# Output weights in the entries of two mixers: late loads behind the next heads, earlier splits, Pool's low parts in pieces of 256 columns, tails by halves

## The chip, the core and the metric

The kernel runs as one program on one core of a Trainium2 chip. The core has a matmul engine (TensorE, PE in the profile; PEld is its loading of stationary tiles), VectorE (DVE), ScalarE (ACT), GpSimd (Pool, POOL) and SyncE (SP, which here issues all DMAs, on one queue). Compute engines work on SBUF (128 partitions) and, all but Pool, on PSUM; each runs its own instruction stream and waits on semaphores. The metric is device microseconds of one execution, median of several runs.

## The reference

One inference step of a two-layer recurrent decoder, width 1024, for a prompt of 1040 tokens (16 of them learned) and for 8 samples of 4 tokens each. Layer 0 has four mLSTM heads and an RG-LRU, layer 1 four heads of gated linear attention (GLA). Each layer is a norm, an input projection, a mixer that carries states, an output projection and a second norm:

```python
hn = _rmsnorm(x, pre_g)
proj = jnp.einsum('bld,de->ble', hn, w_in)
...                                   # layer 0: q, k, v, gates of 4 mLSTM heads; RG-LRU channels
hm = _head_norm(sigmoid(og) * hm, m_norm_g, M_HEADS) * silu(z)
mix = jnp.concatenate([hm, hl * silu(gr)], axis=-1)          # 2048 features
...                                   # layer 1, chunk by chunk
o = qd @ S + causal(qd @ kd.T) @ v
S_new = exp(bL) * S + (k * exp(bL - b)).T @ v
mix = _head_norm(o, g_norm_g, G_HEADS) * silu(r)             # 2048 features
...
out = jnp.einsum('ble,ed->bld', mix, w_out)                  # w_out: 2048 x 1024
y = x + _rmsnorm(out, post_g)
```

All of it is float32, and the new states of prompt and samples are outputs too.

## The kernel before

Five stages stand in a row for each layer's norm, projection and mixer, with barriers between them. A float32 product is made of three products of rounded parts: each operand x is split into a high part (x rounded, a ScalarE copy) and a low part (x minus the high part, a subtraction on VectorE or Pool), and PE multiplies high by high, high by low and low by high.

The mixers (`stage_mix_a` for layer 0, `stage_mix_c` for layer 1) run 36 steps: 9 chunks of 128 tokens (the last holds 16 prompt tokens and the 32 sample tokens) by 4 heads. In step n PE turns and multiplies the next head (`part_a(n + 1)`), makes half of the output projection of head n - 1 (`out(n - 1, 0)`), a unit of the samples' state work (`unit`), the other half (`out(n - 1, 1)`), turns the normed head (`part_c(n)`) and makes the next head's products (`part_b(n + 1)`). Each engine's stream is written out by hand in this order.

SP loads heads two steps ahead into two buffers: step n + 2's head goes when `b_done` says that step n's products are made (`load_head`). At the start of a mixer it loads the second head, the first states, the post-norm row and the residual, some sample inputs, and the late weights.

The output weights (class `OutRing`) are 16 row tiles of 128 x 1024. Some are loaded during the projection (8 in A, 10 in C: `early`), the rest at the start of the mixer (`late`, two tiles, 1 MB, to a DMA: four DMAs in A, three in C; `load_late`). They are split in four groups k of four tiles, in the order in which the first four heads need them: ScalarE makes the four high parts (`split_w_hi`, L1407), VectorE two low parts (`split_w_lo`, L1413), Pool the other two, each in one instruction of 1024 columns (`split_w_lo_pool`, L1420). Group 0 is split before the loop of steps in A and within step 0 in C; group k = n + 1 at the end of step n.

In A, VectorE's chain of a step is: the state's update, the numerator, a division in three small operations on one column (`divide`, L2072 to L2076 with the gating), the norm with ScalarE, the scaling of the normed head (L2082), and the samples' read and update (L2065); PE's `part_c` waits for the scaling and the update. Pool makes the low parts of each head's mix (L2228, L2233) and the masked sample queries (L2238). In C, Pool scales each state after its update (`scale_state`, L3158), makes the mix's low part (`lo`, L3165), and in the beginning builds masks (13 linked operations from L3137 on), the samples' decayed keys (`sample_head`, L3172) and the low parts of six stacks (`stack_lo`, L3204), which PE turns around its first products (`first_turn`, L2801).

The last chunk's output (48 rows) is normed in `tail_act` and `tail_dve`: high and low contributions lie in separate rows of PSUM, ScalarE copies the low ones to SBUF by halves of 512 columns, VectorE adds, ScalarE squares and takes the root, VectorE scales and adds the residual.

Of the kernel before, what the change touches and what calls it, by code (L numbers as in the profile page):

```python
# [21 lines left out]
D = 1024  # L22
# [1332 lines left out]
class OutRing:  # L1355
# [40 lines left out]
    def raw(self, e):  # L1396
        w = self.early if e in self.early.list else self.late
        return w.rows[:, w.list.index(e), :]

    def split_w_hi(self, act, k):  # L1400

        for e in self.order[4 * k:4 * k + 4]:
            if e in self.late.list:
                act.wait_ge(self.late_in[self.late.list.index(e) // 2], 16)
            else:
                act.wait_ge(self.early.loaded, 16 * self.early.tiles // 2)
            act.activation(self.w_hi[:, e, :], self.raw(e), ACT.Copy).then_inc(self.w_hi_ready, 1)  # L1407

# [7 lines left out]
    def split_w_lo_pool(self, pool, k):  # L1416
        for j in range(2, 4):
            e = self.order[4 * k + j]
            pool.wait_ge(self.w_hi_ready, 4 * k + j + 1)
            pool.tensor_tensor(self.w_lo(e), self.raw(e), self.w_hi[:, e, :].bitcast(F32), ALU.subtract  # L1420
                               ).then_inc(self.w_ready_pool, 1)

# [70 lines left out]
    def tail_act(self, act, ps, buf):  # L1493

        for half in range(2):
            act.wait_ge(self.m_used, self.used(4 * NC - 1) - 1 + half)
            act.activation(buf[0:LAST, half * 512:half * 512 + 512], ps[64:64 + LAST, 6 + half, :], ACT.Copy).then_inc(self.tail_low, 1)
        for half in range(2):
            act.wait_ge(self.tail_sum, half + 1)
            act.activation(ps[0:LAST, 6 + half, :], buf[0:LAST, half * 512:half * 512 + 512], ACT.Square,  # L1500
                           accum_out=self.stat[0:LAST, half:half + 1]).then_inc(self.squares, 1)
        self.root(act, 8, LAST)

    def tail_dve(self, dve, ps, buf):
        st = self.stat
        for half in range(2):
            x = buf[0:LAST, half * 512:half * 512 + 512]
            dve.wait_ge(self.tail_low, 2)
            dve.tensor_tensor(x, ps[0:LAST, 6 + half, :], x, ALU.add).then_inc(self.tail_sum, 1)
        dve.wait_ge(self.squares, 18)  # L1510
        dve.tensor_tensor(st[0:LAST, 2:3], st[0:LAST, 0:1], st[0:LAST, 1:2], ALU.add).then_inc(self.sq_sum, 1)
        dve.wait_ge(self.post_rstd, 2 * NC)
        dve.scalar_tensor_tensor(out=buf[0:LAST, :], in0=buf[0:LAST, :], scalar=st[0:LAST, 4:5], in1=self.post[0:LAST, :],
                                 op0=ALU.mult, op1=ALU.mult).then_inc(self.scaled, 1)
        dve.wait_ge(self.scaled, 17)
        dve.wait_ge(self.x_in, 16 * NC)
        dve.tensor_tensor(self.yx[0:LAST, :], buf[0:LAST, :], self.yx[0:LAST, :], ALU.add).then_inc(self.y_ready, 1)

# [37 lines left out]
def stage_mix_a(nc, S, scr_d, lru_d, row_d, w_early, w_late, post_d, x_d, y_d, c0_d, out_cp, out_cs, first):  # L1556
    with ExitStack() as ctx:
# [130 lines left out]
        with nc.Block() as block:  # L1688
            @block.sync
            def _(sp):  # L1690
# [49 lines left out]
                load_state(0)  # L1740
                O.load_late(sp)
                projected(3)
# [5 lines left out]
                for n in range(NSTEP):  # L1748
# [5 lines left out]
                    if n + 1 < UNITS:  # L1754
                        load_state(n + 1)
                    u = unit_of(n)
                    if u is not None:
# [819 lines left out]
def stage_mix_c(nc, S, scr_d, w_early, w_late, post_d, x_d, y_d, s0_d, out_sp, out_ss, first):  # L2577


    with ExitStack() as ctx:  # L2580
# [114 lines left out]
        with nc.Block() as block:  # L2695
            @block.sync
            def _(sp):
# [44 lines left out]
                O.load_x(sp, 0, P)  # L2742
                O.load_late(sp)
                load_sample_r(0)
                load_sample_head(1)
                for n in range(NSTEP):
# [3 lines left out]
                    if n + 2 < NSTEP:  # L2750
                        load_head(n + 2)
                    if 0 < n < UNITS:
                        load_state(n)
# [164 lines left out]
            def _(act):  # L2918
# [62 lines left out]
                def part_m(n):  # L2981
                    c, h, rows = where(n)
                    act.wait_ge(mp_ready, n + 1)
                    if n >= 2:
                        act.wait_ge(O.m_used, O.used(n - 2))
                    x = mp[:].rearrange("p (d t) -> p d t", d=4) if c < 8 else mp8[:, 4 * h:4 * h + 4, :]
                    act.activation(O.hi(n, 0, 4), x, ACT.Copy).then_inc(mhi_ready, 1)
                copy_v(0)
                for j in range(7):
                    if j < 6:  # L2990
                        stack_hi(0, j)
                    if j:
                        aux_copy(0, j - 1)
                for s in range(2):
                    act.wait_ge(S.spilled[s], C_SPILLED[3])
                for n in range(NSTEP):
                    c, h, rows = where(n)
                    norm(n)
                    if n + 1 < NSTEP:
                        copy_v(n + 1)  # L3000
                    if n == 0:
                        O.split_w_hi(act, 0)
                    item = early_aux(n)
# [24 lines left out]
            def _(dve):  # L3028
# [66 lines left out]
                def part_m(n):  # L3095
# [6 lines left out]
                                      ALU.mult).then_inc(mp_ready, 1)  # L3102
                part_a(0)
                dve.wait_ge(pool_chain, POOL_LINKS)
                for n in range(NSTEP):
# [7 lines left out]
                    if n == 0:  # L3113
                        group_keys(0)
                        O.split_w_lo(dve, 0)
                    if u is not None:
# [18 lines left out]
            def _(pool):  # L3135
                link = linker(pool, pool_chain)
                link(pool.memset(qm[:].bitcast(F32), 0.0))  # L3137
                for t in range(3):
                    part = mask_k[t * NS:(t + 1) * NS, :]
                    link(pool.memset(part, 1.0))  # L3140
                    link(pool.affine_select(out=part, in_=part, compare_op=ALU.is_ge, fill=0.0,
                                            base=0, pattern=[[-SLEN, NSEQ]], channel_multiplier=1))
                    link(pool.affine_select(out=part, in_=part, compare_op=ALU.is_ge, fill=0.0,
                                            base=SLEN - 1, pattern=[[SLEN, NSEQ]], channel_multiplier=-1))
                link(pool.memset(mask_s[:], 1.0))
                link(pool.affine_select(out=mask_s[:], in_=mask_s[:], compare_op=ALU.is_ge, fill=0.0,
                                        base=0, pattern=[[1, NS]], channel_multiplier=-1))
                part = mask_s[:].rearrange("p (s t) -> p s t", t=SLEN)
                link(pool.affine_select(out=part, in_=part, compare_op=ALU.is_ge, fill=0.0,
                                        base=0, pattern=[[-SLEN, NSEQ], [0, SLEN]], channel_multiplier=1))  # L3150
                assert link.count() == POOL_LINKS

                def scale_state(n):
# [51 lines left out]
                sample_head(0)  # L3205
                for j in range(6):
                    stack_lo(0, j)
                first_q()
                for n in range(NSTEP):
                    c, h, rows = where(n)  # L3210
                    u = unit_of(n)
                    scale_state(n)
                    if n == 0:
                        O.split_w_lo_pool(pool, 0)
                    if n + 1 < NSTEP:
# [183 lines left out]
```

## Time and profile before

| quantity | value |
| --- | --- |
| median of 3 runs | 2133.11 us (2132.53 to 2135.07) |
| the profiled execution's own time | 2130.55 us |
| its span, first to last instruction | 2128.7 us |
| PE busy | 2037.7 us (96%) |
| DVE / ACT / POOL busy | 1321.2 / 841.3 / 275.3 us |
| mean granted clock of PE | 0.979 of full speed |
| DMA | 264.35 MB, mean 124 GB/s |

Mixer A lies between about 695.6 and 1091 us of the span, mixer C between about 1664.9 us and the end. PE counts as busy while a matmul is in its pipeline, so a busy PE is not PE at its peak. In a timeline a line is one instruction, or several merged (x2, x4), with its start, its duration, and in brackets how long its engine idled before it and what it waited for; an instruction that has started but stands for a memory port counts as busy.

### The profile page before, as it was taken

Reading aid. Unit: us, or ns where it says so; the run is one execution under the profiler, and the core shown is the slowest. Engines: PE = TensorE matmul, PEld = TensorE weight load, DVE = VectorE, ACT = ScalarE, POOL = GpSimd, SP = SyncE. Lnnn points to the kernel's source line nnn. Section 1 sums busy time; section 2 is a strip of 40 time slices with the busy share of each in tenths; the row PEclk is TensorE's granted clock in tenths of the full one; section 3 lists DMA queues with packets and bytes.
Section 4 is the critical chain, followed back from the end, with each engine's and each line's share of the span. In section 5 each row is a group of like instructions: output and inputs, shape, how many; then the busy total and the mean of one; then the engine's idle time right before and its main releaser. Section 6 shows DMA issues by size and latency. Waiting matters only on the chain. (4 is left out here: it accounts for less than half of the span.)

```text
span 2128.7 us, 32848 instructions
## 1 busy us (share of the span) xinstructions
PE 2037.7 (96%) x12606; PEld 1830.4 (86%) x12606; DVE 1321.2 (62%) x2263; ACT 841.3 (40%) x1535; POOL 275.3 (13%) x382
## 2 busy tenths in 40 slices
PE   7999999999999699999959999999999799999998
PEld 7999999999999578788749999999999677777774
DVE  5466676645665676776656656776655576566664
ACT  5555543323231444444455434332212353344333
POOL 0000000000000421111100000000000453333222
PEclk9999999999999799999979999999999899999999
DMA  3121133443343554555332232344333544545442
GB/s 139 55 65 65 53 95 92 132 151 103 101 122 89 204 157 151 161 165 163 102 125 75 81 93 81 121 152 142 107 99 113 183 166 158 180 166 177 161 152 72
DMA packets 209221, 264.35 MB, mean 124 GB/s; under 512 B 48228, under 2 KB 156004, under 8 KB 207032
## 3 DMA queue, kind: packets, MB, share of 16 engines
q1 hardware_dynamic: 209080, 262.42, 38.5%
q8 instruction: 95, 1.56, 0.3%
q14 instruction: 46, 0.38, 0.1%
HBM read 172.39 MB, written 89.99 MB: 123 GB/s over the span
## 5 line engine op out<-in xcount | busy, mean ns | idle before, releaser
L568 DVE TENSOR_TENSOR pa_stage<-pa_ps,pa_stage 128x536 f32<-128x536 f32 x110 | 77.1, 713 | 122.6 <-PE pa_ps L535 112.1
L568 DVE TENSOR_TENSOR pc_stage<-pc_ps,pc_stage 128x536 f32<-128x536 f32 x110 | 77.1, 713 | 98.3 <-PE pc_ps L535 78.3
L382 PE MATMUL pa_ps<-a_XT_hi,pa_w_hi 128*128 128x358 f32 x576 | 133.2, 340 | 0.3 <-PEq L201 0.3
L382 PE MATMUL pa_ps<-a_XT_hi,pa_w_lo 128*128 128x358 f32 x576 | 125.9, 327 | 0.0
L382 PE MATMUL pa_ps<-a_XT_lo,pa_w_hi 128*128 128x358 f32 x576 | 125.8, 326 | 0.0
L535 PE MATMUL pc_ps<-c_XT_hi,pc_w_hi 128*128 128x268 f32 x384 | 110.2, 287 | 0.0
L535 PE MATMUL pa_ps<-a_XT_hi,pa_w_lo 128*128 128x268 f32 x384 | 110.1, 287 | 0.0
L535 PE MATMUL pc_ps<-c_XT_hi,pc_w_lo 128*128 128x268 f32 x384 | 110.1, 287 | 0.0
L535 PE MATMUL pc_ps<-c_XT_lo,pc_w_hi 128*128 128x268 f32 x384 | 110.1, 287 | 0.0
L535 PE MATMUL pa_ps<-a_XT_lo,pa_w_hi 128*128 128x268 f32 x384 | 110.0, 286 | 0.0
L535 PE MATMUL pa_ps<-a_XT_hi,pa_w_hi 128*128 128x268 f32 x384 | 109.8, 286 | 0.0
L1449 PE MATMUL mc_ps<-mc_wout_hi,mc_mix_hi 128*128 128x512 f32 x256 | 105.8, 413 | 2.6 <-POOL mc_mix_lo L3165 2.6
L1449 PE MATMUL ma_ps<-ma_wout_hi,ma_mix_hi 128*128 128x512 f32 x256 | 105.5, 412 | 0.1
L382 PEld LDWEIGHTS pa_ps<-a_XT_hi,pa_w_hi 128*128 128x128 f32 x576 | 100.2, 189 | 5.9 <-issue 0.6
L1449 PE MATMUL ma_ps<-ma_wout_hi,ma_mix_lo 128*128 128x512 f32 x256 | 100.9, 394 | 0.0
L1449 PE MATMUL mc_ps<-mc_wout_hi,mc_mix_lo 128*128 128x512 f32 x256 | 100.8, 394 | 0.0
L1449 PE MATMUL mc_ps<-mc_wout_lo,mc_mix_hi 128*128 128x512 f32 x256 | 100.7, 393 | 0.0
L1449 PE MATMUL ma_ps<-ma_wout_lo,ma_mix_hi 128*128 128x512 f32 x256 | 100.4, 392 | 0.0
L382 PEld LDWEIGHTS pa_ps<-a_XT_hi,pa_w_lo 128*128 128x128 f32 x576 | 99.6, 189 | 0.0
L382 PEld LDWEIGHTS pa_ps<-a_XT_lo,pa_w_hi 128*128 128x128 f32 x576 | 99.4, 189 | 0.0
L3158 POOL TENSOR_TENSOR mc_state<-mc_state,gf 128x512 f32<-128x512 f32 x72 | 75.0, 1062 | 98.3 <-DVE mc_state L3056 98.3
L382 PE MATMUL pc_ps<-c_XT_hi,pc_w_hi 128*128 128x358 f32 x384 | 84.4, 328 | 0.3 <-PEq L201 0.3
(589 smaller groups left out, 6122.7 us busy)
## 6 DMA issues: line engine op xcount, KB each, us to landing
pa_w_raw<-in_w_a SPq DMA_DIRECT2D x57, 512.0 KB, 4.6
pc_w_raw<-in_w_c SPq DMA_DIRECT2D x49, 512.0 KB, 4.5
scr_c<-pc_stage SPq DMA_DIRECT2D x48, 512.0 KB, 3.2
scr_a<-pa_stage SPq DMA_DIRECT2D x40, 512.0 KB, 3.2
mc_sample_state<-in_s SPq DMA_DIRECT2D x32, 512.0 KB, 4.5
out_s_s<-mc_sample_state SPq DMA_DIRECT2D x32, 512.0 KB, 2.7
ma_sample_state<-in_c SPq DMA_DIRECT2D x32, 257.0 KB, 4.1
out_c_s<-ma_sample_state SPq DMA_DIRECT2D x32, 257.0 KB, 2.9
```

The costliest lines, as they stand in the source:

```text
L382: ins = pe.matmul(self.ps[:, 3 * s + t, 0:TC], w[:, k, :], x[:, k, t * TC:(t + 1) * TC], start=(k == 0 and j == 0), stop=(k == KT - 1 and ...
L535: ins = pe.matmul(bank[:, half, :], a[:, k, :], b[:, k, cols], start=(k == 0 and j == 0), stop=(k == KH - 1 and j == 2))
L568: dve.tensor_tensor(dst, self.out(p, product), x, ALU.add).then_inc(self.added, 1)
L1449: ins = pe.matmul(ps[:, 6 + half, :], m[:, at, :], w, start=first and j == 0, stop=last and j == 2)
L3158: ins = pool.tensor_tensor(cst[:, h, d, :], cst[:, h, d, :], factor, ALU.mult)
```

## The change

SP's late loads move behind the loads of step 0 of the loop: in A behind step 2's head and its companions, in C behind step 2's head. Pool's low part of a weight tile is four instructions of 256 columns instead of one of 1024, in both mixers. In C group 0 is split earlier on all three engines: ScalarE's high parts one by one between the copies of the first stacks, VectorE's low parts in front of its wait for the masks, Pool's in front of the loop and so of the first `scale_state`; Pool's decayed keys and its first two stacks stand in front of the masks, and ScalarE's first stack in front of the copy of v. In the tails each half is copied, added, squared and multiplied by the post-norm row on its own, and the last pass over 1024 columns does the root's factor and the residual in one operation. All weights, sums and results are the same; the products by factors are taken in another order in the tails.

```diff
--- before.py
+++ after.py
@@ class OutRing @@
+    def split_w_hi_one(self, act, k, j):
+        e = self.order[4 * k + j]
+        if e in self.late.list:
+            act.wait_ge(self.late_in[self.late.list.index(e) // 2], 16)
+        else:
+            act.wait_ge(self.early.loaded, 16 * self.early.tiles // 2)
+        act.activation(self.w_hi[:, e, :], self.raw(e), ACT.Copy).then_inc(self.w_hi_ready, 1)
+
     def split_w_hi(self, act, k):
...
+        for j in range(4):
+            self.split_w_hi_one(act, k, j)
...
     def split_w_lo_pool(self, pool, k):
         for j in range(2, 4):
             e = self.order[4 * k + j]
             pool.wait_ge(self.w_hi_ready, 4 * k + j + 1)
-            pool.tensor_tensor(self.w_lo(e), self.raw(e), self.w_hi[:, e, :].bitcast(F32), ALU.subtract
-                               ).then_inc(self.w_ready_pool, 1)
+            for cols in (slice(q * D // 4, (q + 1) * D // 4) for q in range(4)):
+                ins = pool.tensor_tensor(self.w_lo(e)[:, cols], self.raw(e)[:, cols], self.w_hi[:, e, cols].bitcast(F32), ALU.subtract)
+            ins.then_inc(self.w_ready_pool, 1)
...
@@ tail_act @@
             act.activation(buf[0:LAST, half * 512:half * 512 + 512], ps[64:64 + LAST, 6 + half, :], ACT.Copy).then_inc(self.tail_low, 1)
-        for half in range(2):
             act.wait_ge(self.tail_sum, half + 1)
...
@@ tail_dve @@
             x = buf[0:LAST, half * 512:half * 512 + 512]
-            dve.wait_ge(self.tail_low, 2)
+            dve.wait_ge(self.tail_low, half + 1)
             dve.tensor_tensor(x, ps[0:LAST, 6 + half, :], x, ALU.add).then_inc(self.tail_sum, 1)
-        dve.wait_ge(self.squares, 18)
+            dve.wait_ge(self.squares, 17 + half)
+            dve.tensor_tensor(x, x, self.post[0:LAST, half * 512:half * 512 + 512], ALU.mult).then_inc(self.scaled, 1)
         dve.tensor_tensor(st[0:LAST, 2:3], st[0:LAST, 0:1], st[0:LAST, 1:2], ALU.add).then_inc(self.sq_sum, 1)
         dve.wait_ge(self.post_rstd, 2 * NC)
-        dve.scalar_tensor_tensor(out=buf[0:LAST, :], in0=buf[0:LAST, :], scalar=st[0:LAST, 4:5], in1=self.post[0:LAST, :],
-                                 op0=ALU.mult, op1=ALU.mult).then_inc(self.scaled, 1)
-        dve.wait_ge(self.scaled, 17)
+        dve.wait_ge(self.scaled, 18)
         dve.wait_ge(self.x_in, 16 * NC)
-        dve.tensor_tensor(self.yx[0:LAST, :], buf[0:LAST, :], self.yx[0:LAST, :], ALU.add).then_inc(self.y_ready, 1)
+        dve.scalar_tensor_tensor(out=self.yx[0:LAST, :], in0=buf[0:LAST, :], scalar=st[0:LAST, 4:5], in1=self.yx[0:LAST, :],
+                                 op0=ALU.mult, op1=ALU.add).then_inc(self.y_ready, 1)
@@ stage_mix_a, sync @@
                 load_state(0)
-                O.load_late(sp)
                 projected(3)
...
                         load_state(n + 1)
+                    if n == 0:
+                        O.load_late(sp)
                     u = unit_of(n)
@@ stage_mix_c, sync @@
                 O.load_x(sp, 0, P)
-                O.load_late(sp)
                 load_sample_r(0)
...
                         load_head(n + 2)
+                    if n == 0:
+                        O.load_late(sp)
                     if 0 < n < UNITS:
@@ stage_mix_c, scalar @@
+                stack_hi(0, 0)
                 copy_v(0)
-                for j in range(7):
+                stack_hi(0, 1)
+                aux_copy(0, 0)
+                for j in range(2, 7):
                     if j < 6:
                         stack_hi(0, j)
-                    if j:
-                        aux_copy(0, j - 1)
+                        O.split_w_hi_one(act, 0, j - 2)
+                    aux_copy(0, j - 1)
...
-                    if n == 0:
-                        O.split_w_hi(act, 0)
@@ stage_mix_c, vector @@
                 part_a(0)
+                O.split_w_lo(dve, 0)
                 dve.wait_ge(pool_chain, POOL_LINKS)
...
                         group_keys(0)
-                        O.split_w_lo(dve, 0)
@@ stage_mix_c, gpsimd: the helpers now stand in front, unchanged @@
+                sample_head(0)
+                for j in range(2):
+                    stack_lo(0, j)
                 link = linker(pool, pool_chain)
                 link(pool.memset(qm[:].bitcast(F32), 0.0))
...
                 assert link.count() == POOL_LINKS
...
-                sample_head(0)
-                for j in range(6):
+                for j in range(2, 6):
                     stack_lo(0, j)
                 first_q()
+                O.split_w_lo_pool(pool, 0)
                 for n in range(NSTEP):
                     c, h, rows = where(n)
                     u = unit_of(n)
                     scale_state(n)
-                    if n == 0:
-                        O.split_w_lo_pool(pool, 0)
```

## Rows read from the trace of the kernel before

**Rows 1.** PE's busy tenths in the 40 slices of the page (53.2 us each).
```profile
PE   7999999999999699999959999999999799999998
```

**Rows 2.** Timeline of PE at mixer A's entry: start us, us, engine line, operation [idle before].
```profile
709.44 0.69 PE L1831 MATMUL ma_ps<-ident,ma_normed 128*128 128x128 f32 x2 [5.47 <-DVE ma_normed L2082]
...
718.25 0.47 PE L1789 MATMUL ma_ps<-ident,first_head_a 128*128 128x128 f32 x1 [2.70 <-DMA first_head_a<-scr_r]
...
728.03 0.38 PE L1831 MATMUL ma_ps<-ident,ma_normed 128*128 128x128 f32 x2
...
741.75 0.66 PE L1831 MATMUL ma_ps<-ident,ma_normed 128*128 128x128 f32 x2 [4.26 <-DVE ma_sample_state L2065]
...
755.76 0.41 PE L1831 MATMUL ma_ps<-ident,ma_normed 128*128 128x128 f32 x2 [2.23 <-DVE ma_sample_state L2065]
```

**Rows 3.** Windows: us, busy of PE, PEld, DVE, ACT, POOL, PEclk, DMA share, GB/s.
```profile
705.00:710.00 5.00, 0.56 (x2) 0.29 (x2) 3.98 (x7) 1.98 (x8) 2.08 (x1) 0.63 1.01 426
```

**Rows 4.** Timeline of SP's issues at mixer A's entry.
```profile
697.74 2.17 SPq L1235 DMA_DIRECT2D wout_a_late<-in_w_oa  x4
...
701.63 10.73 SPq L1722 DMA_DIRECT2D ma_sample_z<-scr_a  x2
712.40 0.47 SPq L1695 DMA_DIRECT2D first_head_a<-scr_a  x1
```

**Rows 5.** Timeline of VectorE in mixer A's steps 0, 1 and 4.
```profile
703.34 1.46 DVE L2072 SCALAR_TENSOR_TENSOR ma_small<-ma_num 128x1 f32<-128x1 f32 x1
704.83 2.26 DVE L2074 TENSOR_TENSOR ma_small<-ma_small,tok 128x1 f32<-128x1 f32 x1
...
725.55 0.86 DVE L2065 SCALAR_TENSOR_TENSOR ma_sample_state<-ma_sample_state,wc,ma_ps 128x257 f32<-128x257 f32 x2
...
759.66 0.16 DVE L2072 SCALAR_TENSOR_TENSOR ma_small<-ma_num 128x1 f32<-128x1 f32 x1
```

**Rows 6.** Timeline of Pool at mixer A's entry.
```profile
700.08 1.21 POOL L2238 CAST ma_q_masked<-first_head_a 128x32 fp32r<-128x32 f32 x1
...
702.44 4.64 POOL L1420 TENSOR_TENSOR ma_wout_lo<-wout_a_early,ma_wout_hi 128x1024 fp32r<-128x1024 f32 x2
710.35 0.72 POOL L2233 TENSOR_TENSOR ma_mix_lo<-ma_hl,ma_mix_hi 128x256 fp32r<-128x256 f32 x1 [3.28 <-ACT ma_mix_hi L1921]
```

**Rows 7.** Timeline of PE at mixer C's entry.
```profile
1669.80 0.66 PE L2801 MATMUL mc_ps<-ident,mc_stack 128*96 128x128 f32 x2 [2.84 <-POOL mc_stack L3204]
...
1684.90 0.44 PE L2787 MATMUL mc_ps<-ident,first_head_c 128*128 128x128 f32 x2 [2.79 <-DMA first_head_c<-scr_c]
...
1689.00 0.79 PE L1449 MATMUL mc_ps<-mc_wout_hi,mc_mix_hi 128*128 128x512 f32 x1 [2.58 <-POOL mc_mix_lo L3165]
```

**Rows 8.** Timelines of ScalarE, Pool and VectorE at mixer C's entry.
```profile
1666.99 0.60 ACT L2925 ACTIVATE mc_v_hi<-mc_ps 128x512 fp32r<-128x512 f32 x1 [21.33 <-PE mc_ps L2793]
...
1664.93 1.01 POOL L3137 MEMSET mc_q_masked<- 128x1088 f32 x1 [567.01 <-POOLq L2344]
...
1668.83 0.30 POOL L3172 TENSOR_TENSOR mc_k_decayed<-first_head_c,gf 128x64 f32<-128x64 f32 x1
...
1681.47 5.27 POOL L1420 TENSOR_TENSOR mc_wout_lo<-wout_c_early,mc_wout_hi 128x1024 fp32r<-128x1024 f32 x2 [2.98 <-ACT mc_wout_hi L1407]
1686.71 2.24 POOL L3165 TENSOR_TENSOR mc_mix_lo<-mc_mix_plain,mc_mix_hi 128x512 fp32r<-128x512 f32 x1
...
1684.45 3.38 DVE L3073 TENSOR_TENSOR mc_sample_state_lo<-mc_sample_state,mc_sample_state_hi 128x1024 fp32r<-128x1024 f32 x1 [1.64 <-ACT mc_sample_state_hi L2958]
```

**Rows 9.** Timelines of ScalarE and VectorE in mixer C's tail.
```profile
2119.88 0.59 ACT L1497 ACTIVATE first_head_c<-mc_ps 48x512 f32<-48x512 f32 x1 [0.33 <-PE mc_ps L1452]
...
2120.50 1.28 DVE L1509 TENSOR_TENSOR first_head_c<-mc_ps,first_head_c 48x512 f32<-48x512 f32 x2 [5.73 <-ACT first_head_c L1497]
...
2123.33 1.28 DVE L1513 SCALAR_TENSOR_TENSOR first_head_c<-first_head_c,mc_post_stat,mc_post 48x1024 f32<-48x1024 f32 x1 [0.60 <-ACT mc_post_stat L1467]
2124.64 1.22 DVE L1517 TENSOR_TENSOR mc_residual<-first_head_c,mc_residual 48x1024 f32<-48x1024 f32 x1
```

More of the change, by code:

```diff
@@ L1398, in raw @@
         return w.rows[:, w.list.index(e), :]
-    def split_w_hi(self, act, k):
[L1402 to L1407, printed above, removed]
+    def split_w_hi_one(self, act, k, j):
[5 more added lines that the diff above has]
+        act.activation(self.w_hi[:, e, :], self.raw(e), ACT.Copy).then_inc(self.w_hi_ready, 1)
+    def split_w_hi(self, act, k):
+        for j in range(4):
+            self.split_w_hi_one(act, k, j)
     def split_w_lo(self, dve, k):
@@ L3135, in _ @@
             def _(pool):
[L3136 to L3151, printed above, removed]
                 def scale_state(n):
@@ L3205, in _ @@
                 sample_head(0)
-                for j in range(6):
+                for j in range(2):
+                    stack_lo(0, j)
+                link = linker(pool, pool_chain)
+                link(pool.memset(qm[:].bitcast(F32), 0.0))
+                for t in range(3):
+                    part = mask_k[t * NS:(t + 1) * NS, :]
+                    link(pool.memset(part, 1.0))
+                    link(pool.affine_select(out=part, in_=part, compare_op=ALU.is_ge, fill=0.0,
+                                            base=0, pattern=[[-SLEN, NSEQ]], channel_multiplier=1))
+                    link(pool.affine_select(out=part, in_=part, compare_op=ALU.is_ge, fill=0.0,
+                                            base=SLEN - 1, pattern=[[SLEN, NSEQ]], channel_multiplier=-1))
+                link(pool.memset(mask_s[:], 1.0))
+                link(pool.affine_select(out=mask_s[:], in_=mask_s[:], compare_op=ALU.is_ge, fill=0.0,
+                                        base=0, pattern=[[1, NS]], channel_multiplier=-1))
+                part = mask_s[:].rearrange("p (s t) -> p s t", t=SLEN)
+                link(pool.affine_select(out=part, in_=part, compare_op=ALU.is_ge, fill=0.0,
+                                        base=0, pattern=[[-SLEN, NSEQ], [0, SLEN]], channel_multiplier=1))
+                assert link.count() == POOL_LINKS
+                for j in range(2, 6):
                     stack_lo(0, j)
                 first_q()
+                O.split_w_lo_pool(pool, 0)
                 for n in range(NSTEP):
```

## Prediction

> **What bounds the kernel now.** Read the busy shares by slice first: the matmul engine PE stands at nine tenths or more but for the first and last slice and three holes: slices 14, 21 and 32 [rows 1]. Slices 14 and 32 hold the entries of the two mixers, which the change touches, so the question is what PE waits for there and whether its next wait lies close behind.
>
> Entry of mixer A: PE idles 5.47 us before the first head's transposes (waiting for VectorE's normed head), 2.70 us for a DMA at step 2's part A, nothing at step 1's transposes, then 4.26 and 2.23 us at steps 2 and 3, ended by VectorE's update of the sample state [rows 2]. From 705 to 710 us the granted clock is 0.63, so part of this stretch runs at 1.2 instead of 2.4 GHz [rows 3].
>
> The DMA wait: SP issues the four late weight loads at 697.74 us, the second sample-z load is then stuck for most of 10.73 us, and step 2's head goes out only at 712.40 [rows 4]. Meanwhile the DMA engines move 426 GB/s [rows 3]: the late weights stand in front.
>
> The VectorE waits: a division on one column takes 1.46 us and the next one 2.26 us, where step 4 has 0.16 for the same line [rows 5]. They start while Pool runs its two low parts of output weights, 2.32 us each [rows 6]; the second division ends at 707.09, with Pool's second piece (702.44 + 4.64 = 707.08). So a VectorE operation with both inputs in SBUF stands until the running Pool operation ends, and gets in between two of them. It also works the other way: Pool's cast of 32 columns, begun while VectorE makes its two low parts, takes 1.21 us [rows 6].
>
> Entry of mixer C: PE waits 2.84 us for Pool's first stack, 2.79 us for a head's DMA and 2.58 us for Pool's low part of the first mix [rows 7]. Pool makes its two low parts of weights from 1681.47 in 5.27 us, and only then the mix's low part (2.24 us, ending at 1688.95); VectorE's low part of a sample state takes 3.38 us meanwhile [rows 8].
>
> **Late loads in A.** Nothing is removed; four issues move behind the loads of step 2's head, row, z and sample state. Step 2's head can go when step 0's products are done, some 10 us earlier than now, with 2.5 MB at most ahead of it; PE asks for it at 715.5 at the earliest. I take the whole 2.70 us as gained. What is late next: the 4.2 MB of late weights take 9.8 us at 426 GB/s, so they land by about 716 us; the splits that read them come a step after that. Queued behind them on SP are step 3's head, which is wanted only after step 2's start, with some 5 us to spare. In C the same move ends the 2.79 us wait, but PE's next wait (Pool's low part) absorbs it: nothing by itself.
>
> **Pieces of 256 columns.** Eight instructions in place of two in each of four groups per mixer. The nearest row for a piece is Pool's own 128x256 subtraction, 0.72 us; a quarter of 2.32 is 0.58 [rows 6]. Between the two, 0.66: a group takes 5.3 instead of 4.64 us. [...]
>
> What VectorE wins: the excess of the two divisions is 1.46 + 2.26 - 2 x 0.16 = 3.4 us. With pieces, the first waits half a piece (0.33), the second a whole one (0.66), the gating behind them and the scaling of the normed head, which now meet pieces too, about 0.45 each: 1.9. I take 1.5 us gained per step. Bounds: with 0.58 and no wait behind the gating 1.1 remain (2.3 gained); with 0.72 and every operation waiting, the reciprocal too, 2.9 (0.5 gained).
>
> On PE's path: step 0 gains 1.5 (its wait ends in this chain), the DMA 2.7, together 4.2. At step 1 VectorE's update ends at 726.41 [rows 5] and PE's transposes start at 728.03 [rows 2], 1.6 us of cover; VectorE itself comes 1.5 + 1.5 earlier, so 4.6 are allowed and the 4.2 stay. Steps 2 and 3 end in VectorE's chain: 1.5 each. Entry of A: 4.2 + 3.0 = 7.2 us. Low: 3.2, cut to 1.6 + 1.0 = 2.6 at step 1, plus 1.0 = 3.6. High: 5.0 + 2.3 + 2.2 = 9.5. From step 4 on PE runs without waits, so what is gained is kept.
>
> **Early splits and Pool's order in C.** ScalarE's four high parts move into the gaps of the first turns, VectorE's two low parts in front of its wait for the masks, Pool's eight pieces in front of the first scaling of the state. The key scaling and two stacks go in front of the masks: PE's 2.84 us wait goes, and its first products can start about 1 us earlier than now, once VectorE has v's low part. But Pool waits for the second stack's high part, which ScalarE makes behind the copy of v (1666.99 to 1667.59), so the masks start at about 1668.1 instead of 1664.93 and still need the 3.9 us that lie before 1668.83 [rows 8], till 1672. VectorE's two low parts (about 2.4 us) now fall upon them. By the cast that took 1.21 [rows 6] the masks' selects wait for these: stack 2 comes at 1674.3, in the middle of PE's first products, which end 1.5 us later than now. Then stacks and first queries till 1678, the pieces till 1683.6, the state's scaling, now in front of the mix (2 us), till 1685.7, and VectorE's low parts of state and weight take the port in between: the first mix's low part is there between 1687 and 1689.3, against 1688.95 today. The 5.6 us that Pool starts earlier are spent on scaling, pieces and contention. I take 0.5 us gained; bounds 2 lost and 4 gained (masks free of VectorE's low parts).
>
> The page SBUF — State Buffer of the Trainium skill (Who interferes with whom) says that the port pair shared by VectorE and GpSimd is an exclusive lock held for a whole instruction, and that a GpSimd instruction which only writes does not contend. By that rule the masks' memsets pass and the selects, which read, stand as I assume; no row here shows a select that met VectorE's low part.
>
> **Tails by halves.** Now both copies end at 2120.47, both sums at 2121.78, and the two last passes take 1.28 + 1.22 us [rows 9]. After: ScalarE squares half 0 before it copies half 1; sum and square (0.64 and about 0.65, with handing over 1.4) take the place of the 0.33 us for which it waits for PE today, so that copy ends 1.05 later; the second sum, behind the first multiplication, ends at 2122.3, 0.55 later; the multiplication of half 1 (0.64) stands in front of the tiny addition that the root waits for; then one pass of 1.28 remains. 0.55 + 0.64 - 1.25 = 0, in both tails; bounds 0.3 either way.
>
> **Sum.** 7.2 + 0.5 + 0 = 7.7 us off the profiled execution's own 2130.55: 2122.9. The median of the runs shown, 2133.11, lies 2.56 above it: 2125.4 us. A measurement of this kernel can tell about 0.2%, 4.3 us, from no change: under 2128.8 is faster.
>
> **Rivals.**
> - The port is freed more fully and the masks are not held up: A gains 9.5, C 3: 2120.6. For it: divisions of 0.16 us slip between two Pool pieces without lengthening them. Against: the cast's 1.21.
> - Mixer C pays: Pool's longer chain and PE's lost time at 1.2 GHz in its longer first wait cost 2 us, while A gains its low 3.6: 2131.5, no change. For it: Pool has scaling and pieces in front of the first mix. Against: Pool starts 5.6 us earlier.
> - The DMA wait moves: step 3's head lands behind the late weights, 2.7 us come back: 2128.1. For it: SP's stuck issue today. Against: the 5 us to spare.
> - Slower: Pool holds the port over its train of pieces, so that a division waits for all eight, at 0.72 each 5.8 us in place of 4.64. That is 1.1 us later on each of VectorE's chains: A's step 1 overruns its cover (2.2 - 1.6 = 0.6), steps 2 and 3 lose 2.2, and C's first two mixes 2: 2133.1 + 4.8 = 2137.9. It decides if the second division still takes over 2.3 us. Against it: today VectorE gets in between two Pool instructions.
>
> **Chances.** Forecast 0.45, fuller gain 0.23, moved wait 0.10 (all three faster); C pays 0.16 (same); train 0.06 (slower). Faster 0.78, same 0.16, slower 0.06. The likeliest case alone spans 2122 to 2128; the range for 8 in 10 reaches from A's and C's high ends (13.5 us) to the low end of A with C losing: 2119 to 2131.
>
> **What the changed profile would show.** Right: no DMA wait at A's step 2, SP issuing that head before the late weights; divisions of 0.3 to 0.9 us in steps 0 to 3, Pool's pieces 0.6 to 0.75; PE's waits at steps 2 and 3 of A shorter by 1.5 to 3 us in sum; step 4 of A about 7 us earlier. In C, Pool's masks stretched to 5 or 6 us and the first mix's low part at about the old time from the stage's start. The tails' last passes one instead of two, and the end no earlier against the last product. Wrong, if the second division keeps over 2 us, if a new DMA wait stands at step 3, or if C's first output products start 3 us earlier or 2 later.

## The result, and the profile after

The changed kernel takes 2121.75 us (median of 4 runs, 2119.16 to 2124.78) against 2134.09 us before: ratio 0.9943, 95% interval 0.993 to 0.9955, 12.3 us faster. The forecast was 2125.4, that is 7.7 us faster, in a range from 2119 to 2131. The profiled execution has a span of 2117.4 us (before 2128.7). Cut at the same marks, the 11.3 us between the two spans lie here (the marks are start times in the timelines, but for two: A's tail ends with its last pass, and the last row with the span):

| stretch | before | after | difference |
| --- | --- | --- | --- |
| start to mixer A's first transpose | 695.63 | 696.37 | +0.74 |
| A's entry: first transpose to step 3's normed head | 60.13 | 48.00 | -12.13 |
| rest of A with its tail | 335.37 | 335.25 | -0.12 |
| layer C's norm and projection | 573.84 | 573.33 | -0.51 |
| mixer C: first transpose to its last product | 454.47 | 455.22 | +0.75 |
| last product to the end | 9.26 | 9.23 | -0.03 |

The first and the fourth row are stretches that the change does not touch; over all profiles here they lie between 694.4 and 696.6, and 573.3 and 577.0. So the gain is A's entry. Mixer C's 0.75 us is less than what the same streams of C differ by between profiles: its entry, to step 3's normed head, took 57.95 us here, 57.57 in a second profile of this kernel and 56.25 in another kernel with the same C (57.22 before).

The page of the changed kernel, PE's slices and the granted clock [rows 1]:

```profile
PE   7999999999999799999969999999999799999998
...
PEclk9999999999999899999979999999999899999999
```

PE's timeline at A's entry, the four normed heads [rows 2]:

```profile
707.13 0.44 PE L1835 MATMUL ma_ps<-ident,ma_normed 128*128 128x128 f32 x2 [2.30 <-DVE ma_normed L2086]
...
721.64 0.41 PE L1835 MATMUL ma_ps<-ident,ma_normed 128*128 128x128 f32 x2 [0.27 <-DVE ma_sample_state L2069]
...
733.00 0.41 PE L1835 MATMUL ma_ps<-ident,ma_normed 128*128 128x128 f32 x2 [1.87 <-DVE ma_sample_state L2069]
...
744.37 0.41 PE L1835 MATMUL ma_ps<-ident,ma_normed 128*128 128x128 f32 x2 [1.87 <-DVE ma_sample_state L2069]
```

The DMA wait is gone, and the steps take 14.51, 11.36 and 11.37 us from head to head where they took 18.59, 13.72 and 14.01. Step 1's output products run at 2.4 GHz almost from the first:

```profile
715.17 0.39 PE L1453 MATMUL ma_ps<-ma_wout_lo,ma_mix_hi 128*128 128x512 f32 x1
```

In before the same product took 0.63 us, which is 1.2 GHz, and PE was back at 0.40 only from 723.4 on:

```profile
720.87 0.63 PE L1449 MATMUL ma_ps<-ma_wout_lo,ma_mix_hi 128*128 128x512 f32 x1
```

SP's issues show why no head is late any more [rows 4]:

```profile
704.01 0.47 SPq L1698 DMA_DIRECT2D first_head_a<-scr_a  x1
...
706.73 2.10 SPq L1235 DMA_DIRECT2D wout_a_late<-in_w_oa  x4
713.38 0.33 SPq L1698 DMA_DIRECT2D ma_hin<-scr_a  x1
```

VectorE's timeline in step 2, and Pool's pieces beside it [rows 5, 6]:

```profile
727.86 0.34 DVE L2076 SCALAR_TENSOR_TENSOR ma_small<-ma_num 128x1 f32<-128x1 f32 x1
728.23 0.66 DVE L2078 TENSOR_TENSOR ma_small<-ma_small,tok 128x1 f32<-128x1 f32 x1
728.92 0.16 DVE L2079 RECIPROCAL ma_small<-ma_small 128x1 f32<-128x1 f32 x1
729.12 0.73 DVE L2080 SCALAR_TENSOR_TENSOR ma_gated<-ma_num,ma_small,ma_og 128x256 f32<-128x256 f32 x1
...
730.99 0.36 DVE L2086 TENSOR_SCALAR ma_normed<-ma_gated,ma_small 128x256 f32<-128x256 f32 x1
```

```profile
726.47 6.15 POOL L1424 TENSOR_TENSOR ma_wout_lo<-wout_a_late,ma_wout_hi 128x256 fp32r<-128x256 f32 x8 [2.63 <-ACT ma_wout_hi L1406]
```

The two divisions take 0.34 and 0.66 us. In the same step of the kernel before they took 1.31 and 2.32:

```profile
734.22 1.31 DVE L2072 SCALAR_TENSOR_TENSOR ma_small<-ma_num 128x1 f32<-128x1 f32 x1
735.56 2.32 DVE L2074 TENSOR_TENSOR ma_small<-ma_small,tok 128x1 f32<-128x1 f32 x1
```

The gating takes 0.73 (0.48 before), the scaling 0.36 (0.35): 2.37 us saved, and the period fell by 2.36.

At C's entry PE and Pool read [rows 7, 8]:

```profile
1662.14 0.31 PE L2806 MATMUL mc_ps<-ident,mc_stack 128*96 128x128 f32 x1 [2.05 <-POOL mc_stack L3193]
...
1675.17 0.48 PE L1453 MATMUL mc_ps<-mc_wout_hi,mc_mix_hi 128*128 128x512 f32 x1
...
1687.73 0.50 PE L1453 MATMUL mc_ps<-mc_wout_hi,mc_mix_hi 128*128 128x512 f32 x1 [1.18 <-POOL mc_mix_lo L3154]
...
1694.38 0.63 PE L1453 MATMUL mc_ps<-mc_wout_lo,mc_mix_hi 128*128 128x512 f32 x1
```

```profile
1657.34 1.06 POOL L3202 TENSOR_SCALAR_AFFINE_SELECT mc_mask_keys<-mc_mask_keys 32x8 f32<-32x8 f32 x1
1658.47 1.19 POOL L3204 TENSOR_SCALAR_AFFINE_SELECT mc_mask_keys<-mc_mask_keys 32x8 f32<-32x8 f32 x1
...
1676.12 6.88 POOL L1424 TENSOR_TENSOR mc_wout_lo<-wout_c_early,mc_wout_hi 128x256 fp32r<-128x256 f32 x8 [1.84 <-ACT mc_wout_hi L1406]
1682.97 2.12 POOL L3147 TENSOR_TENSOR mc_state<-mc_state,gf 128x512 f32<-128x512 f32 x2
...
1686.40 1.27 POOL L3154 TENSOR_TENSOR mc_mix_lo<-mc_mix_plain,mc_mix_hi 128x512 fp32r<-128x512 f32 x1
```

VectorE's low parts of the first weights run beside the two selects:

```profile
1657.12 2.48 DVE L1416 TENSOR_TENSOR mc_wout_lo<-wout_c_early,mc_wout_hi 128x1024 fp32r<-128x1024 f32 x2
```

C starts at 1652.95. The first output products come 22.22 us later (24.03 before), at full clock, and step 1's normed head after 29.81 (32.95): 3.1 us ahead. Then Pool's second group of pieces and the state's scaling stand in front of the second mix's low part; PE waits 1.18 us for it, small waits follow, and from 1694 to 1697.6 its products take 0.63 in place of 0.39 us: 1.2 instead of 2.4 GHz. Step 2's head comes after 45.45 us (45.10 before): in this profile the lead is gone.

The tail, ScalarE's second copy and VectorE's operations [rows 9]:

```profile
2109.65 0.58 ACT L1501 ACTIVATE first_head_c<-mc_ps 48x512 f32<-48x512 f32 x1
```

```profile
2110.38 0.68 DVE L1512 TENSOR_TENSOR first_head_c<-mc_ps,first_head_c 48x512 f32<-48x512 f32 x1
...
2113.20 1.27 DVE L1519 SCALAR_TENSOR_TENSOR mc_residual<-first_head_c,mc_post_stat,mc_residual 48x1024 f32<-48x1024 f32 x1 [0.60 <-ACT mc_post_stat L1471]
```

From the last product's start (2108.17) to the last pass's end are 6.30 us, before 6.42.

### The profile page after: what moved, and what is told of

Same layout as the page of the kernel before. It is cut to its first block and busy times, and to the rows that moved or that the text cites. A ratio compares the mean times of both kernels' runs of the same rounds, so it can differ in the third digit from the quotient of the medians.

```text
span 2117.4 us, 32898 instructions
## 1 busy us (share of the span) xinstructions
PE 2036.4 (96%) x12606; PEld 1828.8 (86%) x12606; DVE 1312.1 (62%) x2265; ACT 840.1 (40%) x1535; POOL 282.6 (13%) x430
```

## The experiments

The theory after the result was that PE at A's entry is held by two chains in turn, SP's late head and VectorE's divisions under Pool's long instructions, so that neither part of the change gives its gain alone; and that in C Pool itself is on PE's path. All times stand beside runs of the kernel before on the same chip. As whole runs of one kernel scatter by several us, the lengths of the entries carry the argument ("entry" is from the mixer's first transpose to step 3's normed head):

| kernel | median us (runs) | ratio to before, 95% interval | A's entry | C's entry |
| --- | --- | --- | --- | --- |
| before | | | 60.13 | 57.22 |
| changed | 2121.75 (4) | 0.9943, 0.993 to 0.9955 | 48.00 | 57.95 |
| late_only | 2130.96 (11) | 0.999, 0.9981 to 0.9999 | 58.10 | 58.15 |
| pieces_only | 2129.7 (11) | 0.999, 0.9978 to 1.0001 | 55.69 | 61.39 |
| c_order_only | 2131.48 (11) | 0.9994, 0.9984 to 1.0004 | 60.41 | 55.30 |
| all_but_c_order | 2125.28 (6) | 0.9965, 0.9953 to 0.9978 | 47.99 | 60.75 |
| c_whole | 2120.01 (4) | 0.993, 0.9913 to 0.9947 | 48.07 | 55.60 |
| c_tiles | 2122.29 (4) | 0.9942, 0.9926 to 0.9959 | 47.99 | 56.66 |
| a_tiles | 2119.61 (4) | 0.9934, 0.9917 to 0.995 | 46.18 | 56.25 |
| memset | 2117.58 (1) | | 45.10 | 53.98 |
| pieces_512 | 2123.69 (1) | | 52.93 | 54.82 |
| pieces_128 | 2124.38 (1) | | 47.07 | 62.88 |
| best | 2116.4 (5) | 0.9922, 0.9908 to 0.9935 | 46.17 | 55.60 |
| after_again | 2122.24 (5) | 0.9946, 0.9933 to 0.996 | 47.97 | 57.57 |

**Late loads alone.** From before, in both mixers:

```diff
-                O.load_late(sp)
...
+                    if n == 0:
+                        O.load_late(sp)
```

> Kernel before with nothing but the moved late loads, in both mixers. Theory of two chains: at mixer A's step 1 PE had waited 2.70 us for the head, but VectorE's update of the sample state ended only 1.6 us before PE wanted it, and steps 2 and 3 end in VectorE's chain; so this move alone gains about 1.6 us, and PE's wait at step 1's transposes appears in the place of the one for the DMA. In mixer C the 2.79 us wait for the head goes and Pool's wait grows by as much: 0. In sum 1 to 2 us faster (2131 to 2132). Rival, parts that add: the wait of 2.70 us and the 1.4 us that the half clock cost behind it are gained whole, 4 us faster.

A's entry is 2.0 us shorter and the kernel 2.2. PE's wait moved to the next releaser, as the two chains have it:

```profile
724.98 0.41 PE L1832 MATMUL ma_ps<-ident,ma_normed 128*128 128x128 f32 x2 [2.79 <-DVE ma_sample_state L2066]
```

The clock came back too. PE still idles 5.48 us before the first normed head here, but with the DMA wait gone it makes step 1's output products at 2.4 GHz:

```profile
716.00 0.40 PE L1449 MATMUL ma_ps<-ma_wout_lo,ma_mix_hi 128*128 128x512 f32 x1
```

**Pieces alone.** From before, the loop over four quarters of a tile in `split_w_lo_pool`, nothing else.

> Kernel before with nothing but Pool's pieces of 256 columns, in both mixers. Theory of two chains: step 0 of mixer A ends 2.3 us earlier, but step 2's head lands when it did, so PE's wait for the DMA grows from 2.70 to about 5 us and step 1 gives the 2.3 us back; steps 2 and 3 gain 2.4 and 2.6 us: 5 us in A. C's first mix comes at most 1 us earlier. In sum 5 us faster (about 2128), and with the kernel of late loads alone clearly less than the 11.4 us by which mixer A's entry is shorter in the changed kernel. Rival, parts that add: 2.3 us in each of four steps, 7 to 9 us faster.

A's entry is 4.4 us shorter, and step 1 gives back what step 0 gained, since the head lands when it did:

```profile
718.55 0.48 PE L1790 MATMUL ma_ps<-ident,first_head_a 128*128 128x128 f32 x1 [5.87 <-DMA first_head_a<-scr_r]
```

Before the first normed head PE idles only 2.08 us in this kernel, yet behind the 5.87 us it makes step 1's first output products at 0.63 us each. So in these profiles the half clock in step 1 goes with the DMA wait.

Alone the two parts take 2.0 and 4.4 us from A's entry, together 12.1: the parts don't add, each uncovers the other's chain. C's entry got 4.2 us longer in this profile, which the expectation did not have; the next run but one shows what pieces do there.

**C's order alone.** From before, the hunks of the scalar, vector and gpsimd streams of mixer C.

> Kernel before with nothing but mixer C's early splits and Pool's new order (whole tiles of 1024 columns, late loads at their old place). Theory that the lead of the entry is given back: the first output products start about 2 us earlier after the mixer's begin, but Pool's two tiles of the next group still stand in front of the second mix's low part, so by the third turn of a normed head the lead is gone; 0 in sum, between 1 us faster and 1 us slower. Rival, lead kept: 2 to 3 us faster.

C's entry is 1.9 us shorter. Here the theory that the lead is given back fell: of 2.9 us at step 1's normed head 1.9 are kept at step 3's. The whole kernel (0.9994) is too coarse to tell it.

**All but C's order.** The changed kernel with those three streams of mixer C as before.

> The changed kernel with mixer C's splits and Pool's order as before (late loads, pieces of 256 and tails as changed). Theory that C's order costs nothing or a little: within 1 us of the changed kernel, that is 11 to 13 us faster than before, mixer C about 0.7 us shorter than in the changed kernel. Rival, C's order brings 2 us or more: only 9 to 10 us faster than before, with PE waiting 2.5 us for the first mix's low part as before.

Missed: 7.9 us faster than before, less than even the rival's 9 to 10, and C's entry takes 60.75 us. Pool, VectorE and PE there:

```profile
1671.07 9.10 POOL L1424 TENSOR_TENSOR mc_wout_lo<-wout_c_early,mc_wout_hi 128x256 fp32r<-128x256 f32 x8 [2.97 <-ACT mc_wout_hi L1406]
```

```profile
1675.49 3.42 DVE L1416 TENSOR_TENSOR mc_wout_lo<-wout_c_early,mc_wout_hi 128x1024 fp32r<-128x1024 f32 x2
```

```profile
1681.44 0.80 PE L1453 MATMUL mc_ps<-mc_wout_hi,mc_mix_hi 128*128 128x512 f32 x1 [5.97 <-POOL mc_mix_lo L3170]
```

Three of the pieces, beside VectorE's long operations, and VectorE's pair in the trace of before:

```profile
1674.44 5.04 POOL L1424 TENSOR_TENSOR mc_wout_lo<-wout_c_early,mc_wout_hi 128x256 fp32r<-128x256 f32 x3
```

```profile
1687.75 5.59 DVE L1413 TENSOR_TENSOR mc_wout_lo<-wout_c_early,mc_wout_hi 128x1024 fp32r<-128x1024 f32 x2
```

Eight pieces take Pool 9.10 us where the two whole tiles took 5.27 [rows 8]; these three took 1.7 us each, where an undisturbed one takes 0.73. VectorE's pair takes 3.42 where it took 5.59: between two pieces VectorE's long operations get in, and Pool waits for each. The kernel of late loads alone, which has the same order in C with whole tiles, waits 3.21 us for the first mix and has an entry of 58.15. Cutting does not remove the contention; it hands the wait to the engine that was cut. In A that is the engine with time to spare, here it is the one PE waits for. C's early order is what keeps these pieces apart from VectorE's pair (5.61 us for group 0 in the changed kernel).

**Whole tiles in C.**

```diff
-    def split_w_lo_pool(self, pool, k):
+    def split_w_lo_pool(self, pool, k, pieces=4):
...
-                O.split_w_lo_pool(pool, 0)
+                O.split_w_lo_pool(pool, 0, pieces=1)
...
-                        O.split_w_lo_pool(pool, n + 1)
+                        O.split_w_lo_pool(pool, n + 1, pieces=1)
```

> The changed kernel with Pool's low parts of mixer C in whole tiles of 1024 columns again, mixer A still in pieces of 256. Theory that pieces hand the port to the other engine: they pay where VectorE is on the path (A) and cost where Pool is (C); mixer C from its first transpose to its last product then takes 452.5 to 453 us, as in the kernel with C's order alone, and not the changed kernel's 455.2; 2 to 3 us faster than the changed kernel, 14 to 15 us faster than before. Rival, pieces are free or good in C as well: C takes 455 us or more.

C's entry takes 55.60 us, about as with the order alone. That is 2.35 less than in the changed kernel's first profile and 1.97 less than in its second, but only 0.65 less than in a_tiles (below), whose streams of C are the changed kernel's. The difference between these profiles is the clock. Behind small waits in step 2 the changed kernel ran some eight output products at 1.2 GHz in both its profiles; a_tiles runs them at 2.4 behind waits alike, and so does this kernel:

```profile
1691.99 0.39 PE L1453 MATMUL mc_ps<-mc_wout_lo,mc_mix_hi 128*128 128x512 f32 x1
```

(The line is from a_tiles.) So at like clock whole tiles are worth 0.65 us here, less than the 2 to 3 of the theory; whether the pieces make the clock fall stays open. To the last product C takes 454.44, not the 452.5 to 453 expected, since one stretch of half clock fell into its last chunk (last section). By the median 1.7 us are gained; with intervals some 7 us wide that alone would not show it.

**One tile behind each mix in C.**

```diff
                     lo(n)
+                    if 0 < n < H:
+                        O.split_w_lo_pool(pool, n, (3,))
                     if n + 1 < H:
-                        O.split_w_lo_pool(pool, n + 1)
+                        O.split_w_lo_pool(pool, n + 1, (2,))
```

> The changed kernel with Pool's order in mixer C's steps changed: of a group, one tile's four pieces stand behind the low part of one mix, the other tile's four behind the low part of the next mix, since PE wants them only for the second half of the output products. Theory that Pool's chain (pieces, scaling, stack, mix) is what PE waits for at the second mix: the wait of 1.18 us goes, the clock does not fall behind it, and mixer C takes 2 to 3 us less than the changed kernel's 455.2. Rival, the lead is lost to VectorE's chain (state copy, low part of scores) and not to Pool's: under 1 us.

The wait at the second mix is gone, but C's entry (56.66) is only 1.3 us shorter than in the changed kernel's first profile, and the changed kernel's own streams of C have given 56.25 (a_tiles), 57.57 and 57.95. At like clock, against a_tiles, nothing is gained. Pool's pieces now run beside VectorE's long operations (8.56 us for eight), and PE waits 1.65 and 1.59 us for VectorE's state copy in steps 2 and 3.

**VectorE's second tile moved in A.** Of `split_w_lo`'s two tiles one goes behind `part_m(n)`:

```diff
                     part_m(n)
+                    if n < H:
+                        O.split_w_lo(dve, n, (1,))
...
                     if n + 1 < H:
-                        O.split_w_lo(dve, n + 1)
+                        O.split_w_lo(dve, n + 1, (0,))
```

> The changed kernel with one of VectorE's two low parts of a group in mixer A moved behind the step's mix, where VectorE idles about 1 us before the sample state's low part. Theory that VectorE's chain still sets steps 2 and 3 (PE waits 1.87 us in each): step periods of 11.37 us become 10.4, the entry of A gets 2 to 3 us shorter, and so does the kernel. Rival, the next wait is right behind (output products waiting for the moved low part, or Pool): under 1 us.

A's entry is 1.8 us shorter, just under the 2 to 3 expected: VectorE's chain was still the bound. Step 2's period is 10.38 us; step 3's is 11.09, with VectorE's two tiles taking 1.34 and 1.75 us beside Pool's sample queries.

**Pool writes, but reads nothing.**

```diff
-            for cols in (slice(q * D // 4, (q + 1) * D // 4) for q in range(4)):
-                ins = pool.tensor_tensor(self.w_lo(e)[:, cols], self.raw(e)[:, cols], self.w_hi[:, e, cols].bitcast(F32), ALU.subtract)
+            ins = pool.memset(self.w_lo(e).bitcast(F32), 0.0)
```

> The changed kernel, but Pool writes zeros over each of its low tiles (one write of 1024 columns, about 1 us, nothing read) in place of subtracting, so two of four low parts of the output weights are left out in both mixers. Theory that VectorE's two-input operations stand for Pool's reads: with nothing read both divisions of steps 0 to 3 in mixer A take 0.16 us though Pool's writes run beside them, and the step period falls by 0.7 to 0.9 us. Rival, any running Pool instruction holds the port: the first division takes up to 1 us. Beside it, the Trainium skill (SBUF — State Buffer, Who interferes with whom) has a GpSimd instruction that only writes as one that does not contend; by that, 0.16 us.

VectorE's divisions begin while Pool's writes (724.34 to 726.24) run, and don't wait:

```profile
725.75 0.16 DVE L2075 SCALAR_TENSOR_TENSOR ma_small<-ma_num 128x1 f32<-128x1 f32 x1
725.94 0.16 DVE L2077 TENSOR_TENSOR ma_small<-ma_small,tok 128x1 f32<-128x1 f32 x1
```

```profile
724.34 1.90 POOL L1423 MEMSET ma_wout_lo<- 128x1024 f32 x2 [2.62 <-ACT ma_wout_hi L1406]
```

The period falls from 11.37 to 10.42 and 10.45 us, that is by the whole rest of the excess. A Pool instruction that writes the same tile but reads nothing is not waited for. The Trainium skill (SBUF — State Buffer, Who interferes with whom) says the same of an instruction that only writes; the trace agrees with 0.16 us.

**Other widths.** 512 and 128 columns in both mixers:

```diff
-            for cols in (slice(q * D // 4, (q + 1) * D // 4) for q in range(4)):
+            for cols in (slice(q * D // 2, (q + 1) * D // 2) for q in range(2)):
```

> The changed kernel with Pool's low parts in pieces of 512 columns, in both mixers. Theory that a two-input operation of VectorE stands until the running Pool instruction ends: the first division waits half a piece, the second a whole one of 1.3 us, so they take about 0.6 and 1.2 us (0.34 and 0.66 with 256 columns, 1.31 and 2.32 with 1024) and the period of mixer A's steps 2 and 3 is 12.0 to 12.4 us (11.37 with 256, 13.7 to 14.0 with 1024). Rival, that Pool slows VectorE by its mean load and not by the instruction: as with 256, 11.4 us.

> The changed kernel with Pool's low parts in pieces of 128 columns, in both mixers. From 1.28 us for 512 columns and 0.74 for 256 a piece is some 0.47 us: the divisions take 0.25 and 0.4, the period of mixer A's steps 2 and 3 falls to about 11.1 us, a group takes Pool 7.5 in place of 6.2 us, and mixer C, where Pool is on the path, gets 2 us longer or more: in sum no better than the changed kernel, 2120 to 2124 us. Rival, smaller pieces go on paying: 2 us faster than the changed kernel.

Second division of step 2 in the kernels of 512 and of 128 columns:

```profile
730.25 1.22 DVE L2078 TENSOR_TENSOR ma_small<-ma_small,tok 128x1 f32<-128x1 f32 x1
```

```profile
727.01 0.39 DVE L2078 TENSOR_TENSOR ma_small<-ma_small,tok 128x1 f32<-128x1 f32 x1
```

With 1024, 512, 256 and 128 columns it takes 2.32, 1.22, 0.66 and 0.39 us, and the period is 13.7 to 14.0, 12.53, 11.37 and 11.1 to 11.4: the wait is one Pool instruction. With 512 the period lies just past the 12.0 to 12.4 expected, since the gating waits for a whole piece too (1.28 us). The first division (0.19 to 0.20 in steps 1 to 3 with 512) starts where a piece ends, so "half a piece" was a mean that these steps don't show. The step-0 group of 4, 8 and 16 pieces takes 5.10, 5.89 and 7.33 us: an estimate from these three is 2.1 ns for a column and 0.18 to 0.20 us for an instruction. In C 128 columns are too many instructions: PE waits 4.14 us for the third mix, and the entry takes 62.88 us.

```profile
1705.03 0.79 PE L1453 MATMUL mc_ps<-mc_wout_hi,mc_mix_hi 128*128 128x512 f32 x1 [4.14 <-POOL mc_mix_lo L3154]
```

**The parts that helped, together.** The edits of c_whole (group 0 left in pieces) and a_tiles:

> The changed kernel with mixer A's moved low part of VectorE and, in mixer C, whole tiles for the groups behind the first one (the first one stays in pieces). Theory: the parts add, since they stand in different mixers; A's entry 46.2 us from its first transpose to step 3's normed head (changed kernel 48.0), C 452.3 to 453 us from first transpose to last product where no stretch at half clock falls into its last chunk (changed kernel 455.2): 4 us faster than the changed kernel run beside it. Rival, C's gain of whole tiles came from the first group: C takes 454 us or more, 2 us faster in sum.

> The changed kernel once more, on the same chip as the best version, for its time beside it: 11 to 13 us faster than before, as in its first runs.

On one chip 2116.4 us against 2122.24: 5.8 us faster than the changed kernel, 17.6 faster than before. A's entry is 46.17 and C's 55.60, as each alone gave. The profiled C took 454.40 to its last product, again with one stretch of half clock in the last chunk. Of the kernels that leave nothing out, pieces of 512 gave the shortest C entry (54.82, one run); joining them with the rest was not tried.

## Why the prediction was right, and what it mis-sized

The time fell into the range, and the mechanism in A is the one foretold. But A's entry gained 12.1 us where 7.2 was said, past the high bound of 9.5, and C's 0.5 can't be told from the scatter of the clock. That the time still lay in the range is in part luck: had C gained as near to its high bound of 4 us as A did to its own, the time would have lain below 2119. The measured 2121.75 is nearer to the rival of the fuller release (2120.6) than to the forecast of 2125.4.

- **Late loads in A: right.** The head goes 7.64 us after the mixer's first transpose instead of 16.77, so 9.1 us earlier (some 10 was said); no DMA wait stands at step 2 or 3, and VectorE's update is the next wait (0.27 us), just covered as reckoned. The term of 2.70 left out the clock behind that wait: in before PE made most of step 1's first output products at half clock. With late loads alone the wait is gone and the clock is full, though the 5.48 us of idling before the first normed head remain; with pieces alone these shrink to 2.08, and half clock still follows the DMA wait. Step 1 fell by 4.08 us.
- **Gain by pieces, 1.5 us a step: mis-sized, 3.05 measured in step 0, 2.36 and 2.64 in steps 2 and 3.** The terms for the divisions (0.33 and 0.66) were the durations that came out (0.34 and 0.66 in step 2), but they were counted as waits on top of 0.16 each; the scaling of the normed head, put at 0.45, lost 0.01, and the gating 0.25 in place of 0.45. What remained was 0.94 us, not 1.9. Step 2 lies just past the high bound of 2.3. Step 3's gain exceeds its wait of 2.23, since behind the wait of 4.26 us the granted clock was 0.50 from 741.75 to 747 in before, and is 1.00 from 733 to 738 now. The four steps came out 1.55, 1.38, 0.86 and 1.14 us above what was summed: 4.93, which is what A's entry gained beyond 7.2.
- **C: 0.5 gained was said; between 1.0 gained and 0.7 lost measured.** These are the entries of 56.25 and 57.95 with the same streams against 57.22 before. Up to the first mix the account holds in kind: the selects stand for VectorE's pair (1.06 and 1.19 us; a memset between VectorE's start and the first select took 0.09), and PE waits 2.05 us for stack 2. The first mix's low part is there 21.3 us after the start, 0.7 before the earliest said (22.0 to 24.3), as VectorE's operations did not get in between. (1678 and 5.3 make 1683.3, not 1683.6.) The chain was followed no further: the second group's pieces, in part beside VectorE's, and the scaling stand before the second mix, and PE waits for it. The lead of 3.1 us at step 1's head (changed kernel's first profile) is 1.0 at step 3's in a_tiles, without the stretch of half clock, and gone in the profiles with it. Group 0 took 5.61 us, near the 5.3 of the sum, but group 1 took 6.88, and without the early order group 0 takes 9.10; a price for a piece without its neighbour's work is not a price for the train.
- **Tails: right.** Second copy 1.05 us later as said (1.04), net 0.12 us gained in C's tail and 0.09 in A's. No run changes the tails alone.
- **Rivals.** The fuller release is what happened in A (12.1), but the masks were held up and C gained no 3 us. "C pays" was right in kind only so far as pieces lengthen Pool's chain. The moved DMA wait did not come. The train that holds the port for eight pieces is refuted in A by 0.66 us; its mirror, that VectorE keeps Pool waiting between pieces, was no rival here and is what all but C's order ran into.

## What to carry to other kernels

Cutting a long instruction that holds a shared resource moves the wait to the engine that was cut: do it where that engine has slack, and look at each stage apart, for the same helper can pay in one and cost in another. When two chains end within a few microseconds of each other, undo the parts one by one before crediting any: here 2.0 and 4.4 us made 12.1. Follow a lengthened chain at least one round past the first wait it removes. And compare lengths at like clock: one stretch of half clock, here 1.3 to 1.8 us, is larger than most terms of such a sum.

## What was not expected of the hardware

The scatter of whole runs has steps. From step 3's normed head to C's last product the profiled runs take 397.2 to 397.3, 398.7 to 398.9 or 400.4 us, whatever the kernel. In the longer ones PE, busy, is granted half the clock for some 3 to 4 us once or twice, each costing about 1.6 us; these stretches lie in the last chunk's output products, some 10, 20 or 44 us before the last one. One in the run with whole tiles in C (window, columns as in [rows 3]):

```profile
2098.79:2102.79 4.00, 4.00 (x11) 2.87 (x11) 1.29 (x2) 1.85 (x5) 2.04 (x2) 0.57 0.00 0
```

Before and the changed kernel both take 397.3 us, so the difference of their spans holds no such stretch of that part. In C's entry the changed kernel has one in both its profiles, behind small waits, and a_tiles, with the same streams and waits, has none. So a change of 1 to 2 us in a kernel like this is read from the stage's own length, and together with its granted clock. What starts such a stretch stays open.
